# A decoder layer with 64 routed experts: three fp32r passes for gate, up and half of down, longer weight runs, skipped padding rows

## The chip, the cores and the metric

The kernel runs on one core of one Trainium2 chip, in one launch. The metric is the device time of that launch in microseconds; lower is better. All weights and activations are float32.

## The reference, cut to what matters

One decoder layer for 512 tokens of width 1024. A token mixer (an RG-LRU branch and an S5 branch from one input projection, joined by gates, one output projection, layer norm) is followed by a mixture of experts, a gated per-layer embedding, and a second layer norm. The change touches the S5 branch's small matmuls and the experts:

```python
combine = jnp.einsum('tk,tke->te', gate, one_hot(expert_idx, 64))   # 8 of 64 experts for each token
y = jnp.einsum('tf,fd->td', silu(xt @ ws_gate) * (xt @ ws_up), ws_down)          # shared expert
for c in range(64 // 8):
    g = jnp.einsum('td,edf->tef', xt, w_gate[sl])      # 1024 -> 256
    u = jnp.einsum('td,edf->tef', xt, w_up[sl])
    hdn = jax.nn.silu(g) * u * combine[:, sl, None]
    y = y + jnp.einsum('tef,efd->td', hdn, w_down[sl]) # 256 -> 1024
```

512 tokens with 8 experts each are 4096 pairs of a token and an expert. The kernel gives each expert one tile of 96 slots (SL), and further overflow tiles only where more than 96 tokens chose it; with these inputs no overflow tile runs.

## The kernel before, in words

Five engines and the DMA queues run their own instruction streams, written out by hand and joined by semaphores; what an engine does next is fixed by the order in its block. SyncE (SP) issues plain loads and stores, GpSimd (POOL) the indirect ones.

*First stage (0 to about 420 us).* The mixer's branches in NB = 4 blocks. In a block TensorE (from L769) does two of x_proj and g_proj(0), turns of U2 and R, the 64-row matmuls K (L802 to L811), g_proj(1), S (L815), g_proj(2), the gates' matmuls (L825, recorded at L833), then Y (L839 to L847: per group g one matmul over 128 rows, L843, and two over 64 rows, L844 and L845), then the next block's x_proj(b+1, 0), then the turn of Y (L855), which waits for Y_kept: four ScalarE copies (L1180) that stand in ScalarE's order behind the gates' sigmoids, the decays (Exp, Tanh, L1171) and the square roots (L1176), which themselves wait for VectorE (L1557) and GpSimd (L570, L572). x_proj and g_proj are already done in three fp32r passes (mm3, L676): a value is split into a high part, its fp32r rounding, and a low part, the rest; high x high, high x low and low x high are added up in PSUM. ScalarE makes the high parts, GpSimd (L536) and VectorE (L1291, called from low) the low ones. A plain fp32 matmul is issued as two instructions, so the 8 products of a 1024-long contraction are x16 in the trace; an fp32r pass is one.

*Second stage (to about 625 us).* The gated products of the mixer, b_product, in three fp32r passes. *Third stage (to about 818 us).* Output projection, layer norm, per-layer embedding, routing, shared expert (sh_in L921, sh_out L962). Routing writes the slot table: GpSimd stores (token, gate) pairs with 32 indirect DMAs (L605), reads the table back (L609), TensorE turns it (L989), and VectorE keeps it (tables_kept, L1748). Unused slots hold the indices T and up, which point at 96 padding rows of x1_dram and acc_dram; those rows are zeroed through yzero (L587, L600).

*Routed experts (from 819 us).* For expert u TensorE's order is gate_up(u) (L1005: 8 products of the rows, as 128x96 weights, with 512 columns of gate and up), x_turn(u+1) (L995), down(u-1) (L1023: two halves of 512 columns, two products each), hid_turn(u) (L1015). ScalarE: silu, half of the row copy (rows_kept), half of the y copy (y_kept). VectorE: the product with up and with the combine weight (L1785), the other halves, and the copy of the turned hidden rows (L1792). Gate, up and down have four buffers each: SP loads expert e+4's gate and up (L465) once g_e_put says that gate_up(e) is done, and its down (L468) after y_e_put. In DRAM a row of gate is 256 values; the buffer interleaves gate and up, so a run is 1 KB; down's runs are 4 KB. GpSimd gathers the 96 rows of expert e+4 (gather, L613) and adds the 96 rows of y to acc_dram (add_rows, L622), one add at a time: each waits for the one before to land. After the last add the sum is reloaded, normed and stored.

The store of acc to acc_dram (L487) is issued when the shared expert is done. The change puts a buffer over acc, and waits for it.

## Time and profile before

| | us |
|---|---|
| three runs | 1622.08, 1614.36, 1612.36 |
| median | 1614.36 |
| the profiled execution | 1616.47 |
| its span, first to last instruction | 1614.6 |
| TensorE busy | 1519.5 (94%) |
| TensorE weight loads busy (beside matmuls) | 855.5 (53%) |
| VectorE busy | 551.5 (34%) |
| ScalarE busy | 339.8 (21%) |
| GpSimd busy | 443.1 (27%) |
| HBM read and written | 297.35 MB, 35.44 MB |

Matmuls are pipelined and their ends are modelled, so the duration of one is longer than the distance to the next; where a rate matters, distances between starts are read. The busy shares are means over stages with different limits, so each part is read from its own stage. PEclk 1.00 is the 2.4 GHz level of TensorE's clock and 0.50 the 1.2 GHz level. DMA share is the mean over the 16 DMA engines of the time that packets took; packets of two queues overlap, so it can pass 1. In the views "issue" is time in which an engine waited for nothing that the profile shows.

### The profile page before, as it was taken

The page shows a single profiled execution, that of the slowest core. Times are in us where ns is not written, and L with a number is a line of the kernel's source. Part 1 is how long each engine was busy: PE and PEld are TensorE (multiplying, and loading weights), DVE is VectorE, ACT ScalarE, POOL GpSimd, SP SyncE. Part 2 cuts the span into 40 slices and gives each one's busy share as a digit, 9 for nine tenths or more (in the row PEclk, how much of TensorE's full clock was granted, in tenths as well). Part 3 has the DMA queues.
Part 4 walks back from the last instruction along what each step waited for, and adds up shares of the span by engine and source line. Part 5 has one row for each costly group of instructions (what it writes and reads, how often), then busy time and mean ns, then how long its engine had stood idle before and what let it go on. Part 6 is the DMA issues. An engine that isn't in the chain of part 4 may idle for free.

```text
span 1614.6 us, 16181 instructions
## 1 busy us (share of the span) xinstructions
PE 1519.5 (94%) x5781; PEld 855.5 (53%) x5781; DVE 551.5 (34%) x920; ACT 339.8 (21%) x527; POOL 443.1 (27%) x416
## 2 busy tenths in 40 slices
PE   7979999999999999999989999999999999999990
PEld 4456767676788886454434444444444444444440
DVE  4597877776410011448211111111111111111114
ACT  4115453537322221010001111111111111111110
POOL 2013433334534432001612222222222222222212
PEclk8999999999999999999999999999999999999996
DMA  8034243442333326700499999999999999999974
GB/s 231 0 118 66 66 66 82 77 77 67 90 93 105 98 85 249 281 14 0 160 331 327 335 326 323 327 341 327 322 318 317 325 327 326 330 330 319 335 228 124
DMA packets 258194, 333.49 MB, mean 207 GB/s; under 512 B 14834, under 2 KB 229570, under 8 KB 249504
## 3 DMA queue, kind: packets, MB, share of 16 engines
q1 hardware_dynamic: 242464, 281.50, 56.1%
q0 software_dynamic: 15680, 51.32, 13.1%
q8 instruction: 32, 0.52, 0.1%
q14 instruction: 18, 0.15, 0.0%
HBM read 297.35 MB, written 35.44 MB: 206 GB/s over the span
## 4 chain that ended last, share of the span: by engine, by line
PE 69%; DMA 13%; issue 6%; DVE 4%; POOL 3%; SPq 3%; ACT 1%; POOLq 1%; DVEq 1%; ACTq 0%
PE bank L1011 20%; DMA arena<-moe_w_up_in 12%; PE bank L1030 10%; PE bank L677 6%; PE bank L678 6%; PE bank L679 6%; PE bank L684 4%; PE bank L905 3%; PE bank L891 3%; PE bank L711 3%; POOL wa_low L536 2%; SPq L468 2%; PE bank L925 2%; DVE arena L1291 1%; DVE lru_low L1291 1%
## 5 line engine op out<-in xcount | busy, mean ns | idle before, releaser
L1011 PE MATMUL bank<-arena 128*96 128x512 f32 x1024 | 455.2, 598 | 20.4 <-DMA arena<-moe_w_up_in 19.4
L1088 ACT ACTIVATE arena<-bank 128x512 f32<-128x512 f32 (+6 forms) x312 | 163.3, 543 | 859.5 <-PE bank L1011 442.0
L1011 PEld LDWEIGHTS bank<-arena 128*96 128x96 f32 x1024 | 164.0, 165 | 265.4 <-issue 265.3
L1030 PE MATMUL bank<-arena 128*96 128x512 f32 x512 | 230.4, 592 | 1.0 <-DVE arena L1792 1.0
L1291 DVE TENSOR_TENSOR arena<-arena 128x512 f32<-128x512 f32 (+10 forms) x286 | 206.7, 754 | 31.3 <-POOLq L561 12.7
L1297 DVE SCALAR_TENSOR_TENSOR arena<-arena,bank 96x256 f32<-96x256 f32 (+1 forms) x72 | 36.0, 500 | 482.3 <-ACT arena L1088 451.4
L684 PEld LDWEIGHTS bank<-arena 96*128 96x128 f32 (+4 forms) x1001 | 127.9, 186 | 83.9 <-issue 82.5
L536 POOL TENSOR_TENSOR wb_low<-arena,wb_high 128x1024 fp32r<-128x1024 f32 (+1 forms) x40 | 106.5, 2665 | 149.9 <-ACT wb_high L1088 149.9
L626 POOL COPY arena<-arena 96x1 int32 (+1 forms) x64 | 11.5, 180 | 468.3 <-DVE arena L1780 423.3
L684 PE MATMUL bank<-arena 96*128 96x96 f32 (+4 forms) x1001 | 128.4, 267 | 10.6 <-DMA arena<-x_in 4.7
L1030 PEld LDWEIGHTS bank<-arena 128*96 128x96 f32 x512 | 80.3, 167 | 103.9 <-issue 103.9
L536 POOL TENSOR_TENSOR wa_low<-arena,wa_high 128x1024 fp32r<-128x1024 f32 x24 | 61.8, 2591 | 197.4 <-ACT wa_high L1088 197.4
L629 POOL DMA_INDIRECT acc_dram<-arena x64 | 94.3, 1473 | 55.1 <-POOL arena L626 50.5
L1780 DVE COPY arena<-bank 96x512 f32<-96x512 f32 x64 | 44.0, 687 | 185.3 <-PE bank L1030 167.8
L677 PE MATMUL bank<-x_high,wa_high 128*128 128x512 f32 x192 | 77.4, 403 | 8.1 <-DVE x_low L1291 7.9
L1297 DVE SCALAR_TENSOR_TENSOR arena<-bank,arena 128x511 f32<-128x511 f32 (+3 forms) x44 | 32.2, 747 | 139.5 <-PE bank L679 137.3
L1088 ACT ACTIVATE wb_high<-arena 128x1024 fp32r<-128x1024 f32 (+1 forms) x40 | 45.8, 1145 | 147.1 <-DMA arena<-w_glu_in 81.6
L678 PE MATMUL bank<-x_low,wa_high 128*128 128x512 f32 x192 | 75.4, 392 | 0.0
L679 PE MATMUL bank<-x_high,wa_low 128*128 128x512 f32 x192 | 75.3, 392 | 0.0
L618 POOL DMA_INDIRECT arena<-x_dram,arena x64 | 60.5, 945 | 51.6 <-POOL arena L615 51.6
L1088 ACT ACTIVATE arena<-arena 128x512 f32<-128x512 f32 (+5 forms) x54 | 32.0, 610 | 181.7 <-DVE arena L1597 88.0
L605 POOL DMA_INDIRECT slot_dram<-arena x32 | 31.8, 992 | 130.6 <-DVEq L1288 121.1
(146 smaller groups left out, 1758.0 us busy)
## 6 DMA issues: line engine op xcount, KB each, us to landing
arena<-moe_w_gate_in SPq DMA_DIRECT2D x64, 1024.0 KB, 14.2
arena<-moe_w_up_in SPq DMA_DIRECT2D x64, 1024.0 KB, 19.0
...
arena<-w_in_in SPq DMA_DIRECT2D x2, 2048.0 KB, 11.9
```

What stands on the lines that cost most here:

```text
L536: nc.gpsimd.tensor_tensor(lo, w, hi.bitcast(f32), ALU.subtract).then_inc(S["w_split"], 1)
L618: nc.gpsimd.indirect_dma_start(out=xg[u], out_offset=None, in_=x1_dram, in_offset=bass.IndirectOffsetOnAxis(ap=idxcol[:, u:u + 1].bitcast( ...
L629: nc.gpsimd.indirect_dma_start(out=acc_dram, out_offset=bass.IndirectOffsetOnAxis(ap=idxcol[:, 4:5].bitcast(u32), axis=0), in_=yb[buf], in ...
L677: mm(dst, w_hi, v_hi, start=start, stop=False)
L678: mm(dst, w_hi, v_lo, start=False, stop=False)
L679: return mm(dst, w_lo, v_hi, start=False, stop=stop)
L684: return nc.tensor.transpose(dst, src, ident[0:n, 0:n])
L1011: last = mm(banks[2 + u % 2][0:SL, :], xgT[u % 2][:, k, :], gu[u % 4][:, k, :, :], start=(k == 0), stop=(k == KD - 1))
L1030: last = mm(banks[5 + hf][0:SL, :], hT[u % 2][:, k, 0:SL], dn[u % 4][:, k, hf * 512:(hf + 1) * 512], start=(k == 0), stop=(k == 1))
L1088: return nc.scalar.activation(out_, in_, func, **kw)
L1291: return V_.tensor_tensor(out_, a, b_, op)
L1297: return V_.scalar_tensor_tensor(out_, a, s, b_, op0, op1)
```

## The change

- Gate, up and the first half (k = 0) of down's contraction go in three fp32r passes. Per expert ScalarE makes the high parts: four copies of 128x1024 for gate and up (gate_up_high), one for down (down_high), two of 128x384 for the rows (rows_high), one of 128x96 for the hidden rows; VectorE makes the low parts by subtraction in the same shapes, for the weights in place (gate_up_low, down_low, rows_low). The second half of down stays fp32. The high parts of gate and up have two buffers, the second over acc, so ScalarE waits for acc_stored ahead of its first expert; the turned rows have one buffer. gate_up_high(u+1) and gate_up_low(u+1) stand at the head of expert(u) on their engines.
- Gate, up and down are loaded in runs of 8 KB; the buffers of gate and up are no longer interleaved. This holds for the shared expert too.
- Padding rows are skipped: gather and add have a bounds check at T-1; the padding rows and their zeroing are gone, and GpSimd zeroes the four gather buffers once (96x4096), between slot_ready and the 32 stores of the slot table.
- On GpSimd the add of expert u-1 stands behind the gather of u+4, in place of the add of u.
- K's and Y's matmuls are reordered: Y does its 16 matmuls over 128 rows first, then the 64-row ones with the two halves of rows in turn; K likewise takes the halves in turn.

Its core (the rename of semaphores, the overflow branch and declarations are left out; `plain` is `part` with type float32):

```diff
-        gu = [at(o, KD * 2 * F).rearrange("p (k w f) -> p k w f", k=KD, w=2)
-              for o in (b1, tail, late + 4096, b0)]
-        dn = [at(o, 2 * D).rearrange("p (k c) -> p k c", k=2)
-              for o in (b1 + 4096, b0 + 6144, b1 + 6144, b0 + 4096)]
+        gu_at = (b1, tail, late + 4096, b0)
+        gu_raw = [plain(f"gate_up{n}", o, 2 * KD, F) for n, o in enumerate(gu_at)]
+        gu = [v.rearrange("p (w k) f -> p k w f", w=2) for v in gu_raw]
+        gu_row = [[v[:, w * KD:(w + 1) * KD, :].rearrange("p k f -> p (k f)") for w in range(2)] for v in gu_raw]
+        dn_at = (b1 + 4096, b0 + 6144, b1 + 6144, b0 + 4096)
+        dn = [plain(f"down{n}", o, 2, D) for n, o in enumerate(dn_at)]
+        dn_row = [v.rearrange("p k c -> p (k c)") for v in dn]
         xg = [at(late + n * D, D, SL) for n in range(4)]
-        xgT = [at(b1 + 8192 + n * KD * SL, KD * SL).rearrange("p (k s) -> p k s", k=KD) for n in range(2)]
+        xg_all = at(late, 4 * D, SL)
+        xgT = at(tail + 4096, KD * SL).rearrange("p (k s) -> p k s", k=KD)
+        xe_hi = part("rows_high", tail + 4096, KD, SL)
+        xe_lo = part("rows_low", tail + 4096 + KD * SL, KD, SL)
+        gu_hi = [part(f"gate_up_high{n}", o, 2 * KD, F) for n, o in enumerate((x_off, m_off))]
+        gu_lo = [part(f"gate_up_low{n}", o, 2 * KD, F) for n, o in enumerate(gu_at)]
+        dn_hi = [part(f"down_high{n}", o, 2, D) for n, o in enumerate((b1 + 8192, sg_off))]
+        dn_lo = [part(f"down_low{n}", o, 2, D) for n, o in enumerate(dn_at)]
+        he_hi = [part(f"hidden_high{n}", b1 + 10240 + 512 * n, 1, SL)[:, 0] for n in range(2)]
+        he_lo = [part(f"hidden_low{n}", b1 + 10240 + 512 * n + 128, 1, SL)[:, 0] for n in range(2)]
...
             def load_in(e, u, done):
                 for w, src in enumerate((w_gate_e, w_up_e)):
-                    sp.dma_start(gu[u][:, :, w, :], src[bass.ds(e, 1)].rearrange("o p k f -> p (o k) f")).then_inc(done, 16)
+                    sp.dma_start(gu_row[u][w], src[bass.ds(e, 1)].rearrange("o p x -> p (o x)")).then_inc(done, 16)
 
             def load_down(e, u, done):
-                sp.dma_start(dn[u], w_down_e[bass.ds(e, 1)].rearrange("o p k c -> p (o k) c")).then_inc(done, 16)
+                sp.dma_start(dn_row[u], w_down_e[bass.ds(e, 1)].rearrange("o p x -> p (o x)")).then_inc(done, 16)
...
+            pool.wait_ge(S["padded"], 16)
+            pool.wait_ge(S["res_put"], 2 * TT)
             pool.wait_ge(S["slot_ready"], 1)
+            nc.gpsimd.memset(xg_all, 0.0)
+            pool.drain()
             for t in range(TT):
                 for k in range(K):
                     nc.gpsimd.indirect_dma_start(
...
                 nc.gpsimd.indirect_dma_start(
                     out=xg[u], out_offset=None, in_=x1_dram,
-                    in_offset=bass.IndirectOffsetOnAxis(ap=idxcol[:, u:u + 1].bitcast(u32), axis=0)).then_inc(s_gath[u], 16)
+                    in_offset=bass.IndirectOffsetOnAxis(ap=idxcol[:, u:u + 1].bitcast(u32), axis=0),
+                    bounds_check=T - 1, oob_is_err=False).then_inc(s_gath[u], 16)
...
                 pool.sem_inc(S["col_seen"], 1)
                 nc.gpsimd.indirect_dma_start(
                     out=acc_dram, out_offset=bass.IndirectOffsetOnAxis(ap=idxcol[:, 4:5].bitcast(u32), axis=0),
-                    in_=yb[buf], in_offset=None, compute_op=ALU.add).then_inc(S["rows_added"], 16)
+                    in_=yb[buf], in_offset=None, bounds_check=T - 1, oob_is_err=False,
+                    compute_op=ALU.add).then_inc(S["rows_added"], 16)
...
             for u in range(4):
                 pool.wait_ge(S["xT_e_put"], u + 1)
                 gather(4 + u, u, 4 + u)
-                add_expert(0, u)
+                if u:
+                    add_expert(0, u - 1)
             with pool.Fori(1, E // 4 - 1) as i:
                 for u in range(4):
                     pool.wait_ge(S["xT_e_put"], 4 * i + (u + 1))
                     gather(4 * i + (4 + u), u, 4 * i + (4 + u))
-                    add_expert(i, u)
+                    add_expert(i, u - 1)
             for u in range(E - 4, E):
-                add_expert(0, u)
+                add_expert(0, u - 1)
+            add_expert(0, E - 1)
...
-                for g in range(GB):
-                    q, h = divmod(g, 2)
-                    hs = slice(h * NS, (h + 1) * NS)
-                    if g == 0:
-                        pe.wait_ge(S["RT_kept"], 4 * (b + 1))
+                pe.wait_ge(S["RT_kept"], 4 * (b + 1))
+                for q in range(QB):
                     for c in range(2):
-                        last = mm(banks[4 + 2 * h + q // 4][0:GP, (q % 4) * P:(q % 4 + 1) * P], bT[hs, c, b * QB + q, :],
-                                  Q[hs, c, q, 0:L, :], start=(c == 0), stop=(c == 1))
-                    if g % 8 == 7:
+                        for h in range(2):
+                            hs = slice(h * NS, (h + 1) * NS)
+                            last = mm(banks[4 + 2 * h + q // 4][0:GP, (q % 4) * P:(q % 4 + 1) * P],
+                                      bT[hs, c, b * QB + q, :], Q[hs, c, q, 0:L, :], start=(c == 0), stop=(c == 1))
+                    if q % 4 == 3:
                         last.then_inc(S["K_put"], 1)
...
-                for g in range(GB):
-                    q, h = divmod(g, 2)
-                    hs = slice(h * NS, (h + 1) * NS)
-                    dst = banks[4 + 2 * h + q // 4][0:NC, (q % 4) * P:(q % 4 + 1) * P]
-                    mm(dst, U[:, g, :], M[:, g, :], start=True, stop=False)
-                    mm(dst, hp[hs, 0, q, 0:NC], Q[hs, 0, q, 1:L + 1, :], start=False, stop=False)
-                    last = mm(dst, hp[hs, 1, q, 0:NC], Q[hs, 1, q, 1:L + 1, :], start=False, stop=True)
-                    if g % 8 == 7:
-                        last.then_inc(S["Y_put"], 1)
+                for q in range(QB):
+                    for h in range(2):
+                        mm(y_bank(h, q), U[:, 2 * q + h, :], M[:, 2 * q + h, :], start=(q % 4 == 0), stop=False)
+                for j in range(2):
+                    for c in range(2):
+                        for q in range(4 * j, 4 * j + 4):
+                            for h in range(2):
+                                hs = slice(h * NS, (h + 1) * NS)
+                                last = mm(y_bank(h, q), hp[hs, c, q, 0:NC], Q[hs, c, q, 1:L + 1, :],
+                                          start=False, stop=(c == 1 and q % 4 == 3))
+                    last.then_inc(S["Y_put"], 1)
...
             def gate_up(i, u):
 
-                pe.wait_ge(s_wgu[u % 4], 32 * i + 32 * (u // 4 + 1))
-                pe.wait_ge(S["xT_e_act"], 4 * i + u + 1)
-                pe.wait_ge(S["xT_e_dve"], 4 * i + u + 1)
+                pe.wait_ge(S["gu_e_low"], 16 * i + 4 * u + 4)
+                pe.wait_ge(S["xT_e_low"], 8 * i + 2 * u + 2)
+                whi = gu_hi[u % 2].rearrange("p (w k) f -> p k w f", w=2)
+                wlo = gu_lo[u % 4].rearrange("p (w k) f -> p k w f", w=2)
                 for k in range(KD):
-                    last = mm(banks[2 + u % 2][0:SL, :], xgT[u % 2][:, k, :], gu[u % 4][:, k, :, :],
-                              start=(k == 0), stop=(k == KD - 1))
+                    last = mm3(banks[2 + u % 2][0:SL, :], xe_hi[:, k], xe_lo[:, k], whi[:, k], wlo[:, k], k == 0, k == KD - 1)
                 last.then_inc(S["g_e_put"], 1)
 
...
 
             def down(i, u):
-                pe.wait_ge(s_wdn[u % 4], 16 * i + 16 * (u // 4 + 1))
-                pe.wait_ge(S["hT_e_kept"], 4 * i + u + 1)
+                pe.wait_ge(S["dn_e_low"], 4 * i + u + 1)
+                pe.wait_ge(S["hT_e_high"], 8 * i + 2 * u + 2)
+                pe.wait_ge(S["hT_e_low"], 4 * i + u + 1)
                 wait(pe, S["y_e_act"], 4 * i + u)
                 wait(pe, S["y_e_dve"], 4 * i + u)
                 for hf in range(2):
-                    for k in range(2):
-                        last = mm(banks[5 + hf][0:SL, :], hT[u % 2][:, k, 0:SL], dn[u % 4][:, k, hf * 512:(hf + 1) * 512],
-                                  start=(k == 0), stop=(k == 1))
+                    hs = slice(hf * 512, (hf + 1) * 512)
+                    mm3(banks[5 + hf][0:SL, :], he_hi[u % 2], he_lo[u % 2], dn_hi[u % 2][:, 0, hs], dn_lo[u % 4][:, 0, hs],
+                        True, False)
+                    last = mm(banks[5 + hf][0:SL, :], he[u % 2], dn[u % 4][:, 1, hs], start=False, stop=True)
                 last.then_inc(S["y_e_put"], 1)
 
...
-            def rows_kept(i, u):
+            def rows_high(i, u):
                 act.wait_ge(S["xT_e_put"], 4 * i + u + 1)
-                f(xgT[u % 2][:, 0:4, :], banks[0][:, 0:4 * SL].rearrange("p (k x) -> p k x", k=4), ACT.Copy).then_inc(S["xT_e_act"], 1)
+                for h in range(2):
+                    f(xe_hi[:, 4 * h:4 * h + 4], banks[h][:, 0:4 * SL].rearrange("p (k x) -> p k x", k=4),
+                      ACT.Copy).then_inc(S["xT_e_high"], 1)
+
+            def gate_up_high(i, u):
+                act.wait_ge(s_wgu[u % 4], 32 * i + 32 * (u // 4 + 1))
+                wait(act, S["g_e_put"], 4 * i + u - 1)
+                for k in range(2):
+                    for w in range(2):
+                        ks = slice(KD * w + 4 * k, KD * w + 4 * k + 4)
+                        f(gu_hi[u % 2][:, ks], gu_raw[u % 4][:, ks], ACT.Copy).then_inc(S["gu_e_high"], 1)
+
+            def down_high(i, u):
+                act.wait_ge(s_wdn[u % 4], 16 * i + 16 * (u // 4 + 1))
+                wait(act, S["y_e_put"], 4 * i + u - 1)
+                f(dn_hi[u % 2][:, 0], dn[u % 4][:, 0], ACT.Copy).then_inc(S["dn_e_high"], 1)
 
...
 
             def expert(i, u, more=True):
+                if more:
+                    gate_up_high(i, u + 1)
                 act.wait_ge(S["g_e_put"], 4 * i + u + 1)
-                wait(act, S["hid_e"], 4 * i + u - 1)
-                f(sil[u % 2][0:SL, :], banks[2 + u % 2][0:SL, 0:F], ACT.Silu).then_inc(S["silu_e"], 1)
+                wait(act, S["hT_e_put"], 4 * i + u - 1)
+                f(hid_e[u % 2], banks[2 + u % 2][0:SL, 0:F], ACT.Silu).then_inc(S["silu_e"], 1)
                 if more:
-                    rows_kept(i, u + 1)
+                    rows_high(i, u + 1)
+                down_high(i, u)
                 if not isinstance(i, int) or u >= 1:
                     y_kept(i, u - 1)
-
-            rows_kept(0, 0)
+                act.wait_ge(S["hT_e_put"], 4 * i + u + 1)
+                wait(act, S["y_e_put"], 4 * i + u - 1)
+                f(he_hi[u % 2], banks[4][:, 0:SL], ACT.Copy).then_inc(S["hT_e_high"], 1)
+                f(he[u % 2], banks[4][:, SL:2 * SL], ACT.Copy).then_inc(S["hT_e_high"], 1)
+
+            act.wait_ge(S["slot_ready"], 1)
+            gate_up_high(0, 0)
+            rows_high(0, 0)
+            act.wait_ge(S["acc_stored"], 16)
             for u in range(0, 5):
                 expert(0, u)
...
-            def rows_kept(i, u):
-                dve.wait_ge(S["xT_e_put"], 4 * i + u + 1)
-                V_.tensor_copy(xgT[u % 2][:, 4:8, :], banks[1][:, 0:4 * SL].rearrange("p (k x) -> p k x", k=4)).then_inc(S["xT_e_dve"], 1)
+            def rows_low(i, u):
+                for h in range(2):
+                    ks = slice(4 * h, 4 * h + 4)
+                    dve.wait_ge(S["xT_e_high"], 8 * i + 2 * u + h + 1)
+                    tt(xe_lo[:, ks], banks[h][:, 0:4 * SL].rearrange("p (k x) -> p k x", k=4), xe_hi[:, ks].bitcast(f32),
+                       ALU.subtract).then_inc(S["xT_e_low"], 1)
+
+            def down_low(i, u):
+                dve.wait_ge(S["dn_e_high"], 4 * i + u + 1)
+                tt(dn_lo[u % 4][:, 0], dn[u % 4][:, 0], dn_hi[u % 2][:, 0].bitcast(f32), ALU.subtract).then_inc(S["dn_e_low"], 1)
+
+            def gate_up_low(i, u):
+                for k in range(2):
+                    for w in range(2):
+                        ks = slice(KD * w + 4 * k, KD * w + 4 * k + 4)
+                        dve.wait_ge(S["gu_e_high"], 16 * i + 4 * u + 2 * k + w + 1)
+                        tt(gu_lo[u % 4][:, ks], gu_raw[u % 4][:, ks], gu_hi[u % 2][:, ks].bitcast(f32),
+                           ALU.subtract).then_inc(S["gu_e_low"], 1)
...
             def expert(i, u, more=True):
+                if more:
+                    gate_up_low(i, u + 1)
                 dve.wait_ge(S["silu_e"], 4 * i + u + 1)
-
-                stt(hdn[u % 2][0:SL, :], sil[u % 2][0:SL, :], gateT[:, bass.ds(4 * i + u, 1)],
+                stt(hid_e[u % 2], hid_e[u % 2], gateT[:, bass.ds(4 * i + u, 1)],
                     banks[2 + u % 2][0:SL, F:2 * F], ALU.mult, ALU.mult).then_inc(S["hid_e"], 1)
                 if more:
-                    rows_kept(i, u + 1)
+                    rows_low(i, u + 1)
+                down_low(i, u)
                 if not isinstance(i, int) or u >= 1:
                     y_kept(i, u - 1)
-                dve.wait_ge(S["hT_e_put"], 4 * i + u + 1)
-                V_.tensor_copy(hT[u % 2][:, :, 0:SL], banks[4][:, 0:2 * SL].rearrange("p (k x) -> p k x", k=2)).then_inc(S["hT_e_kept"], 1)
-
-            rows_kept(0, 0)
+                dve.wait_ge(S["hT_e_high"], 8 * i + 2 * u + 2)
+                tt(he_lo[u % 2], banks[4][:, 0:SL], he_hi[u % 2].bitcast(f32), ALU.subtract).then_inc(S["hT_e_low"], 1)
+
+            gate_up_low(0, 0)
+            rows_low(0, 0)
             for u in range(0, 5):
                 expert(0, u)
```

## Rows read from the trace of the kernel before

**Rows 1.** The page, 40 slices of the span: GB/s moved by DMA in each.

```profile
GB/s 231 0 118 66 66 66 82 77 77 67 90 93 105 98 85 249 281 14 0 160 331 327 335 326 323 327 341 327 322 318 317 325 327 326 330 330 319 335 228 124
```

**Rows 2.** Chain of waits, start of the routed experts: start us, us, what.

```profile
806.79 3.71 PE bank L978 x8
...
821.51 9.27 PE bank L1011 x16
...
832.37 7.08 PE bank L1011 x16
...
840.30 3.44 PE bank L1030 x8
...
843.94 6.87 PE bank L1011 x16
```

**Rows 3.** Chain of waits, end of the execution: expert 63's last gate/up matmul ends.

```profile
1570.41 3.45 PE bank L1030 x8
```

**Rows 4.** Stages: us, busy (x) PE PEld DVE ACT POOL, PEclk, DMA share, GB/s.

```profile
614.00:622.00 8.00, 8.00 (x37) 6.61 (x36) 0.46 (x1) 1.97 (x2) 1.52 (x1) 1.00 1.02 415
780.00:790.00 10.00, 8.96 (x23) 4.10 (x22) 2.04 (x4) 0.38 (x1) 7.76 (x8) 1.00 1.08 369
820.00:825.00 5.00, 4.26 (x9) 1.71 (x8) 0.56 (x1) 0.49 (x1) 0.10 (x1) 0.50 1.09 317
850.00:1150.00 300.00, 300.00 (x902) 133.01 (x901) 50.42 (x106) 38.87 (x80) 72.82 (x104) 1.00 1.07 330
1150.00:1550.00 400.00, 380.50 (x1120) 167.82 (x1119) 62.64 (x132) 48.23 (x99) 91.26 (x130) 1.00 1.07 325
```

**Rows 5.** Waits, 850 to 1560 us: us in total, times, longest.

```profile
PE bank L1011 <- DMA arena<-moe_w_up_in: 19.4, 23, 1.9
```

**Rows 6.** TensorE in order of time, product with w_lru_out: 24 matmuls between.

```profile
560.08 0.39 PE L677 MATMUL bank<-s_high,wb_high 128*128 128x512 f32 x1
...
565.52 0.39 PE L677 MATMUL bank<-lru_high,wb_high 128*128 128x512 f32 x1
```

**Rows 7.** DMA queues, 1150 to 1550 us: packets, MB, share of 16 engines.

```profile
q1 hardware_dynamic: 73481, 103.93, 79.9%
q0 software_dynamic: 7391, 25.94, 26.6%
```

**Rows 8.** Groups by form, whole execution: busy us, mean ns, idle before.

```profile
L1088 ACT ACTIVATE wb_high<-arena 128x1024 fp32r<-128x1024 f32 x32 | 33.9, 1059 | 115.9 <-DMA arena<-w_glu_in 81.6 <-DMA arena<-w_in_in 34.3
...
L1291 DVE TENSOR_TENSOR arena<-arena 128x1024 f32<-128x1024 f32 x43 | 51.6, 1223 | 3.1 <-issue 0.9
...
L1775 DVE COPY arena<-bank 128x384 f32<-128x384 f32 x64 | 35.1, 548 | 3.0 <-PE bank L684 3.0
...
L1291 DVE TENSOR_TENSOR lru_low<-arena,lru_high 128x512 fp32r<-128x512 f32 x12 | 17.2, 1503 | 0.0
```

**Rows 9.** The page, DMA issues: queue, count, KB each, us from issue to landing.

```profile
acc_dram<-arena SPq DMA_DIRECT2D x1, 2048.0 KB, 16.4
...
acc_dram<-arena POOLq DMA_INDIRECT x64, 8.8
```

**Rows 10.** GpSimd, then VectorE, in order of time: zeroing, token table, shared expert's end.

```profile
630.48 0.95 POOL L587 MEMSET arena<- 96x1024 f32 x1
...
804.15 0.62 POOL L609 DMA_DIRECT2D arena<-slot_dram  x1 [1.42 <-DMA slot_dram<-arena]
...
816.50 1.28 DVE L1291 TENSOR_TENSOR arena<-arena,bank 128x512 f32<-128x512 f32 x2 [3.79 <-PE bank L978]
```

**Rows 11.** Block 1 in order of time: K, Y's first, next product, Y's copies.

```profile
193.42 3.68 PE L808 MATMUL bank<-arena 64*16 64x128 f32 x64 [0.94 <-ACT arena L1088]
...
222.40 0.43 PE L843 MATMUL bank<-arena 128*64 128x128 f32 x2
...
237.44 0.50 PE L677 MATMUL bank<-x_high,wa_high 128*128 128x512 f32 x1
...
240.68 2.04 ACT L1088 ACTIVATE arena<-bank 64x512 f32<-64x512 f32 x4
```

65 lines of the change are left out of this document (34 added, 31 removed).

## The prediction

> **What bounds the kernel now.** I read the 40 slices of the page first: the last 31 of them, from about 760 us on, hold a stretch in which the DMA engines move 320 to 340 GB/s without a break [rows 1]. That is the routed experts. The chain of waits through their start gives the beat: gate and up of one expert are 16 fp32 instructions in 6.87 us, the turn of the next rows 0.86 (from 839.45, the end of one gate/up, to 840.30), down 3.44, the turn of the hidden rows 0.20 (from 843.74 to 843.94), so 11.37 us of TensorE per expert, back to back [rows 2]. From expert 1's first gate/up matmul (832.37) to expert 63's last (1570.41 [rows 3]) there are 62 periods and one gate/up: (738.0 - 6.9) / 62 = 11.79 us. The stages say who sets it: TensorE is busy for all of 850 to 1150, but for only 380.5 of the 400 us after it, while the DMA share stays at 1.07 [rows 4]; the missing 19.4 us are waits for moe_w_up [rows 5]. One expert moves 3 x 1.049 MB of weights and 2 x 0.393 MB of gathered and scattered rows, 3.93 MB; at 325 GB/s that is 12.1 us. So DMA at 12.1 is the limit, TensorE at 11.37 lies just under it, and the buffers hide the difference for the first 26 experts (26 x 0.7 = 18 us). Both must fall for the time to fall.
>
> **TensorE per expert, after.** An fp32 instruction takes 6.87 / 16 = 0.429 us, two per product. An fp32r product of the same 512 columns comes every (565.52 - 560.08) / 24 = 0.227 us [rows 6]. Gate/up becomes 24 x 0.227 = 5.45. Down becomes 6 x 0.227 for the first half of its contraction and 4 x 0.429 for the second, 3.08. The turns stay, 1.06. Sum 9.59 us, against 11.37. With 96 weight columns in place of 128 the 0.227 may be a little less; 0.2135, half of an fp32 instruction, gives 9.18, the lower end.
>
> **DMA per expert, after.** Queue 1 moves 260 GB/s (103.9 MB in 400 us) in a share of 0.799, queue 0 65 GB/s in 0.266: 325 and 244 GB/s per unit of share, 1.065 in all [rows 7]. With expert loads almost alone (1 KB runs for two thirds of the bytes) the trace shows 369 at 1.08, or 342 per unit; with the 4 KB runs of w_out alone 415 at 1.02, or 407 [rows 4]. I carry over the same loss beside queue 0 (325/342 = 0.95): 8 KB runs then go at 387 per unit, 3.146 / 387 = 8.13 us. 512 tokens in 8 experts each are 4096 rows, 64 per expert of 96, and no overflow tile ran, so skipping leaves 0.524 MB: 2.15 us. (8.13 + 2.15) / 1.065 = 9.65 us. Bounds: nothing lost beside queue 0, 9.3; runs of no effect and only the skipping, (9.68 + 2.15) / 1.065 = 11.1; neither effect, 12.1. I take 9.65, since rows at both run lengths exist.
>
> **ScalarE and VectorE per expert.** In 850 to 1150 they are busy 38.9 and 50.4 us over 26.4 experts, 1.47 and 1.91 each [rows 4]. ScalarE gains four highs of gate/up and one of down at 1.06, one more row copy at 0.55 (VectorE's for the same shape), and two 96-column copies (estimate 0.3 each, under the 0.55 for 384 columns): 1.47 + 5.3 + 0.55 + 0.6 = 7.9 us. VectorE gains five lows at 1.22 and one more half of the rows at 0.55; the hidden copy only changes: 1.91 + 6.1 + 0.55 = 8.6 us [rows 8]. Both are under 9.6. What matters too is the loop through them, since each runs in order: down(u-1) ends, y copy 0.6, hidden copies 0.6, first high 1.06, four lows 4.9, gate product 0.48, two row lows 1.1, some 0.4 of semaphores: 9.1 us to the start of gate/up(u+2). TensorE takes 0.2 + 5.45 + 0.86 + 3.08 + 0.2 = 9.8 for the same stretch. 0.7 us are left, so the lows are hidden, but a low of 1.4 us in place of 1.22 would no longer be. The serial scatter is as close: 8.8 us to landing plus some 1.0 us of column copy and semaphore [rows 9] is 9.8 at 96 rows; for 64 rows the 8.8 lies between two thirds of it, 5.9, and all of it, and I take 7.5, so 8.5. Deferring it by one expert on GpSimd costs nothing: two y buffers cover it.
>
> With three limits between 9.1 and 9.7 they disturb each other; buffers hide some 18 us of DMA lag as before. I take a period of 9.8 us.
>
> **The start of the routed stage.** gate_up_low(0,0) stands on VectorE behind the shared expert (done at 817.8 [rows 10]): four lows to 822.7, row lows to 823.8, so gate/up(0) starts at 823.9 and not 821.5. Then ScalarE waits for acc_stored before it may write the high parts of expert 1 over acc. That store is issued at 821.0 and takes 16.4 us to land [rows 9], 837.4; ahead of it were the loads of experts 2 and 3, which now go faster, so I take 833.5. Then four highs (4.2), silu 0.4, product after the last low 1.7, row lows 1.1: gate/up(1) starts at 840.6, 8.2 later than 832.37. TensorE idles some 8 us and restarts at the lower clock: after the gap at 819 the granted clock was 0.50 in 820 to 825 [rows 4], the 1.2 GHz level, and gate/up(0) took 9.27 in place of 6.87 [rows 2]. I add 2. The memset of 96x4096 before the 32 token stores is 4 x 0.95 = 3.8 us [rows 10]; the token table's read, issued by 804.8 and landed some 2 us later (my estimate), then lands at about 810.6, and TensorE asks for it at 810.5 [rows 2, 10], so 0 (if that cover is gone, up to 4 us). The dropped zero stores were off the path.
>
> **K and Y by row halves.** K: 64 instructions in 3.68 us, 0.0575 each; a 128-column fp32 instruction at the rate of the long ones would be 0.107, so the halves overlap already, and reordering gives 0 (at most 3.68 - 64 x 0.0535 = 0.3 per block). Y: 16 groups from 222.40 to 237.44, 0.94 us each. New: 32 full instructions at 0.107 and 64 half ones at K's rate, 3.4 + 3.7 = 7.1 us in place of 15.0. But what follows is x_proj(b+1,0), 5.45 us, and then the turn of Y, which waits for ScalarE's four copies, 240.68 to 242.72: their start comes from the chain of decays and square roots, not from Y [rows 11]. TensorE arrived at 242.9 before, and will arrive at 235.0 and wait 7.7 us. So of 4 x 7.9 = 32 us, 0.2 per block remain, and the idle time costs a restart at the lower clock, 1 to 3 us each (the shape of 820 to 825). Net for this stage: +3 us (bounds -4 and +10). The shared expert only changes its layout.
>
> **Sum.** Expert 63's gate/up ends at 842.6 + 62 x 9.8 + 5.45 = 1455.7; first stage +3; tail as before 1614.6 - 1570.4 = 44.2. Span 1502.9. The profiled execution took 1616.47, 1.87 outside its span, and lies 2.1 above the median of 1614.36: 1502.9 + 1.9 - 2.1 = 1502.7, say **1502 us**. In general: 895 + 62T.
>
> **The rivals.**
> - *DMA stays the bound* (0.17): 8 KB runs bring less beside gathers. T of 10.3 to 10.9 after the buffers' share: 1534 to 1571. For it: 1.07 all along; the 415 was without queue 0. Against: the sum above. A cap on all traffic together, whatever its runs, is the same rival seen otherwise: at 350 GB/s, midway between the 330 of the routed stage and the 369 of loads alone [rows 4], 3.67 MB take 10.5 us, less 0.3 hidden 10.2, and the time is 1527; 0.05 of the 0.17, since w_out's load reached 415. The Trainium skill states such a cap (DMA: Bandwidth & Descriptors, Specifications): HBM gives a core about 358 GB/s; by it 3.67 MB would take 10.25 us. If skipped rows cost as before (the change not doing what it says), (8.13 + 3.22) / 1.065 = 10.7, less 0.3 hidden: 1540.
> - *The loop of ScalarE and VectorE, or the scatter* (0.17): lows at 1.4 to 1.6 us, or 9.8 of scatter kept whole with GpSimd held up. T 10.1 to 10.8: 1521 to 1565. For it: VectorE 90% full, in strict order.
> - *Faster than forecast* (0.08): 9.18 of TensorE and DMA near 9.3, T 9.35: 1475.
> - *Slower than before* (0.05): lows lengthened by GpSimd beside them. The lru_low lows, 0.68 us alone, took 1.50 on average beside GpSimd's subtractions [rows 8]. At T = 11.6 the gain is gone; that is lows of (11.6 - 2.5) / 5 = 1.8 us. At twice the price, 2.4, T = 14.5 and the time is 1794. Against it: beside experts GpSimd runs only one-column copies and descriptor writing.
> - *The forecast*, T 9.5 to 10.1: 0.53.
>
> **How the numbers follow.** Range 1476 to 1562: it leaves out the slower rival and the ends of the others. Faster by over 1% (about what a measurement of this kernel can tell from no change) takes all but the slow rival and T between 11.3 and 11.9: 0.92; within 1% 0.04; slower 0.04.
>
> **What would show it.** Right: gate/up in 5.3 to 5.5 us, down near 3.1, rate near 375 GB/s, period 9.6 to 10, gate/up(1) starting some 8 us later, Y near 7 us followed by a TensorE wait for ScalarE of 7 to 8 us. Wrong: TensorE waiting for VectorE's gate_up_low at each expert (loop), ScalarE waiting for moe_w_up (DMA), lows above 1.4 us, or a first stage shorter by over 5 us.

## The result, and the profile after

The kernel after the change takes 1589.7 us (median of four runs, 1586.16 to 1593.05) where the kernel before takes 1614.3: a ratio of 0.983, 95% interval 0.980 to 0.986. The direction was forecast, the size was not: 1502 us was given, with 1562 as the upper end. The profiled execution has a span of 1591.2 us, 88.3 above the 1502.9 of the sum.

The page of the kernel after, slices and queues [rows 1]:

```profile
PEclk7999898989999999999997999999999999999995
DMA  8034242425133334810246999999999999999953
GB/s 235 0 106 80 67 68 67 67 54 106 53 106 99 86 106 165 330 76 1 84 170 211 344 348 344 336 333 337 323 337 328 332 340 322 334 326 330 325 147 118
DMA packets 141492, 315.98 MB, mean 199 GB/s; under 512 B 18898, under 2 KB 100514, under 8 KB 116160
...
gate_up<-moe_w_gate_in SPq DMA_DIRECT2D x64, 1024.0 KB, 12.4
gate_up<-moe_w_up_in SPq DMA_DIRECT2D x64, 1024.0 KB, 26.2
```

Packets fell from 258194 to 141492 and the bytes from 333.5 to 316.0 MB, so both DMA parts do what they say; yet the routed stage still moves 330 GB/s and not 375. (The prediction speaks of the last 31 slices of the page before; from 760 us on it is some 21 of them.)

Stages after, columns as in [rows 4]:

```profile
850.00:1150.00 300.00, 274.58 (x1188) 179.96 (x1188) 218.01 (x273) 187.62 (x304) 92.09 (x104) 0.98 0.92 322
1150.00:1450.00 300.00, 276.74 (x1189) 178.70 (x1188) 212.72 (x272) 182.31 (x298) 93.56 (x108) 1.00 0.94 331
```

TensorE now idles 8%, and the DMA share is 0.94 where it was 1.07. Nothing in this row looks full. The waits of the same 300 us (us in total, times, longest):

```profile
POOL arena L647 <- DMA acc_dram<-arena: 156.4, 27, 6.3
DVE gate_up_low L1346 <- ACT gate_up_high L1118: 86.8, 27, 3.7
ACT gate_up_high L1118 <- DMA gate_up<-moe_w_up_in: 79.6, 27, 3.4
ACT arena L1118 <- DMA acc_dram<-arena: 38.1, 27, 2.4
```

Two things are late at every expert: the add of the expert before (POOL and ScalarE's y copy wait for it) and the up weights (ScalarE's high parts wait for them, and VectorE and TensorE behind it). The chain of waits names only the first; it ended

```profile
1498.29 8.95 DMA acc_dram<-arena
1507.47 1.10 POOL arena L647
1508.71 0.51 issue
1509.45 9.28 DMA acc_dram<-arena
1518.96 0.36 POOL arena L647
```

and says 37% of the whole span is adds landing. From one add to the next: about 9.1 us of landing and 1.8 of copy, semaphores and issue, 10.9, which is the period. From this I took theory A, that the serial chain of adds sets the period. It was wrong, as two_acc shows below.

The start of the routed experts, TensorE and ScalarE in order of time (start us, us, ..., idle before):

```profile
827.23 1.03 PE L707 MATMUL bank<-arena 106*96 106x106 f32 x4 [5.75 <-DMA arena<-slot_dram]
...
841.00 0.71 PE L700 MATMUL bank<-gate_up_high,rows_high 128*96 128x512 f32 x1 [4.42 <-DVE rows_low L1346]
...
854.26 3.90 ACT L1118 ACTIVATE gate_up_high<-gate_up 128x1024 fp32r<-128x1024 f32 x4 [16.77 <-DMA acc_dram<-arena]
...
861.46 0.71 PE L700 MATMUL bank<-gate_up_high,rows_high 128*96 128x512 f32 x1 [0.43 <-DVE rows_low L1346]
```

The token table is 5.75 us late, and ScalarE waits 16.77 us for the accumulator's store before it may write the high parts of expert 1.

The 88.3 us come apart by the prediction's own steps. Gate/up of expert 1 starts at 861.46, the sum had 845.6: 15.9. Gate/up of expert 63 starts at 1539.21, so the period is (1539.21 - 861.46) / 62 = 10.93 and not 9.8: 70.1. Its own length and the tail, 1591.2 - 1544.8 = 46.4 for 44.2: 2.3.

### The profile page after: what moved, and what is told of

It reads as the page before. It is cut to its first block, busy times and chain, and to the rows that moved or that the text cites. A ratio compares the mean times of both kernels' runs of the same rounds, so it can differ in the third digit from the quotient of the medians.

```text
span 1591.2 us, 19168 instructions
## 1 busy us (share of the span) xinstructions
PE 1422.4 (89%) x6421; PEld 958.7 (60%) x6421; DVE 921.3 (58%) x1304; ACT 678.3 (43%) x1039; POOL 493.1 (31%) x414
## 2 busy tenths in 40 slices
DMA packets 141492, 315.98 MB, mean 199 GB/s; under 512 B 18898, under 2 KB 100514, under 8 KB 116160
## 4 chain that ended last, share of the span: by engine, by line
DMA 38%; PE 36%; issue 8%; POOL 6%; DVE 5%; ACT 2%; POOLq 2%; DVEq 1%; SPq 0%; ACTq 0%
DMA acc_dram<-arena 37%; PE bank L700 8%; PE bank L701 7%; PE bank L702 7%; PE bank L918 3%; POOL arena L647 3%; PE bank L734 3%; POOL slot_dram L625 2%; DVE arena L1346 2%; PE bank L707 2%; PE bank L932 2%; ACT arena L1118 1%; POOLq L591 1%; PE bank L833 1%; POOL arena L592 1%
## 5 line engine op out<-in xcount | busy, mean ns | idle before, releaser
L1346 DVE TENSOR_TENSOR gate_up_low<-gate_up,gate_up_high 128x1024 fp32r<-128x1024 f32 x256 | 296.5, 1221 | 193.4 <-ACT gate_up_high L1118 193.4
L1118 ACT ACTIVATE gate_up_high<-gate_up 128x1024 fp32r<-128x1024 f32 x256 | 249.7, 1048 | 178.7 <-DMA gate_up<-moe_w_up_in 161.9
L700 PE MATMUL bank<-gate_up_high,rows_high 128*96 128x512 f32 x512 | 208.4, 407 | 29.1 <-DVE rows_low L1346 29.1
L702 PE MATMUL bank<-gate_up_high,rows_low 128*96 128x512 f32 x512 | 203.9, 398 | 0.0
L701 PE MATMUL bank<-gate_up_low,rows_high 128*96 128x512 f32 x512 | 202.5, 396 | 0.0
L647 POOL COPY arena<-arena 96x1 int32 (+1 forms) x64 | 46.9, 733 | 375.9 <-DMA acc_dram<-arena 360.3
L1061 PE MATMUL bank<-down,arena 128*96 128x512 f32 x256 | 130.6, 592 | 0.0
L700 PEld LDWEIGHTS bank<-gate_up_high,rows_high 128*96 128x96 f32 x512 | 83.6, 163 | 69.6 <-DVE rows_low L1346 31.5
L702 PEld LDWEIGHTS bank<-gate_up_high,rows_low 128*96 128x96 f32 x512 | 83.4, 163 | 36.8
L701 PEld LDWEIGHTS bank<-gate_up_low,rows_high 128*96 128x96 f32 x512 | 83.8, 164 | 32.5
```

What stands on the lines that cost most here:

```text
L647: nc.gpsimd.tensor_copy(idxcol[:, 4:5].bitcast(i32), idxT[:, bass.ds(e, 1)].bitcast(i32)).then_inc(S["sc_col"], 1)
L700: mm(dst, w_hi, v_hi, start=start, stop=False)
L701: mm(dst, w_hi, v_lo, start=False, stop=False)
L702: return mm(dst, w_lo, v_hi, start=False, stop=stop)
L1061: last = mm(banks[5 + hf][0:SL, :], he[u % 2], dn[u % 4][:, 1, hs], start=False, stop=True)
L1118: return nc.scalar.activation(out_, in_, func, **kw)
```

## The experiments

Fifteen runs in four groups; a ratio is to the kernel before on the same chip, with its 95% interval. The chips differ by up to 1.2% (1614.3 to 1633.0 us for the kernel before), so kernels of different groups are compared by ratio. The period P is the time between adds, from 950 to 1450 us (first to last issue over their number less one); by that measure the kernel before has 11.87 and the kernel after 11.09 (10.93 over the whole stage, since the first experts live on loaded buffers).

| kernel | us | ratio (interval) | P |
|---|---|---|---|
| the kernel after | 1589.7 | 0.983 (0.980 to 0.986) | 11.09 |
| no_add | 1525.7 | 0.934 (0.930 to 0.939) | 9.74 |
| two_acc | 1608.9 | 0.986 (0.981 to 0.991) | 11.08 |
| y_old | 1597.1 | 0.978 (0.973 to 0.982) | 11.19 |
| short_runs | 1600.6 | 0.981 (0.976 to 0.986) | 11.14 |
| half_down | 1530.2 | 0.935 (0.930 to 0.940) | 9.73 |
| pad_rows | 1603.9 | 0.981 (0.978 to 0.985) | 11.25 |
| interleaved | 1631.1 | 1.000 (0.998 to 1.003) | 11.60 |
| before_dma | 1604.9 | 0.982 (0.979 to 0.986) | 11.37 |
| spread | 1534.2 | 0.951 (0.947 to 0.955) | 10.21 |
| start_fix | 1570.5 | 0.974 (0.970 to 0.978) | 11.08 |
| best3 | 1512.2 | 0.937 (0.933 to 0.940) | 10.18 |
| best3_again | 1526.7 | 0.937 (0.934 to 0.940) | 10.14 |
| best4 | 1536.1 | 0.942 (0.939 to 0.946) | 10.18 |
| pad_spread | 1605.6 | 0.984 (0.980 to 0.988) | 11.19 |
| before_spread | 1603.3 | 0.983 (0.979 to 0.986) | 11.36 |

(no_add issues no adds; its P is from the first high part of expert 1, at 863.2, to that of expert 63, at 1467.4.)

**First group: is it the chain of adds?** The kernel before took 1633.0 us on this chip.

no_add:

```diff
-                nc.gpsimd.indirect_dma_start(out=acc_dram, ..., compute_op=ALU.add).then_inc(S["rows_added"], 16)
+                pool.sem_inc(S["rows_added"], 16)
```

> The kernel after the change without the transfer that adds an expert's rows into the accumulator in DRAM (its semaphore is raised by GpSimd itself; the output then lacks the routed experts' part). Theory A: the period of 10.93 us an expert is the serial chain of these adds (landing 9.1 us, then 1.8 us until the next is issued). Without them the period falls to what TensorE needs, 9.6 to 9.9 us, and the whole to 1510 to 1530 us. Rival B: the experts' weights arrive too late, or ScalarE's and VectorE's loop is longer than worked out: the period stays at 10.6 us or more and the whole at 1565 us or more.

1525.7 us, P 9.74; TensorE is busy for all 300 us of the stage. A's numbers, but the run took two things away together, the chain and the adds' traffic. What the traffic is, the queues' shares from 1150 to 1450 us show, after first, then no_add:

```profile
q1 hardware_dynamic: 11710, 85.28, 75.4%
q0 software_dynamic: 6063, 13.94, 18.9%
```

```profile
q1 hardware_dynamic: 13290, 96.82, 85.8%
q0 software_dynamic: 3472, 8.03, 8.3%
```

16 x 300 x 0.189 us over 1.70 thousand rows moved each way (13.94 MB in rows of 4 KB, half of them adds) and 16 x 300 x 0.083 over 1.96 thousand gathered alone give 0.20 us of an engine for a gathered row and some 0.33 for an added one, against 0.35 for 8 KB of weights. An added row costs as much as twice its bytes of weights.

two_acc:

```diff
-    out=acc_dram, out_offset=...idxcol[:, 4:5]...).then_inc(S["rows_added"], 16)
+    out=(acc_dram, acc2_dram)[par], out_offset=...idxcol[:, 4 + par:5 + par]...).then_inc(s_add[par], 16)
```

> The kernel after the change with the same adds, going by turns into two accumulators in DRAM, each with its own semaphore and column of indices, so that an add waits for the one before the last. The second accumulator is zeroed by 2 MB of stores ahead of the experts, read back at the end and added on VectorE. All the traffic of the adds stays. Theory A (the serial chain): period 9.7 to 10.2 us, the whole 1530 to 1560 us, some 3 us of it for the zeroing and the last sum. Rival B (the adds' traffic, the weights or the engines' loop bound the period): 10.7 us or more, the whole 1585 us or more.

1608.9 us, P 11.08: B's numbers. The chain is gone, and ScalarE waits for the weights in its place, 105.5 us where it was 79.6:

```profile
POOL arena L653 <- DVE arena L1856: 157.8, 27, 7.4
ACT gate_up_high L1125 <- DMA gate_up<-moe_w_up_in: 105.5, 27, 4.9
```

So the chain that the view showed was a follower: the serial adds fill the period they are given. Why one add takes 9 us to land is another question, and no run answers it: in before_dma below it takes 9.6 us at a DMA share of only 0.89.

short_runs:

```diff
-  sp.dma_start(gu_row[u][w], src[bass.ds(e, 1)].rearrange("o p x -> p (o x)"))
+  sp.dma_start(gu_raw[u][:, w * KD:(w + 1) * KD, :], src[bass.ds(e, 1)].rearrange("o p k f -> p (o k) f"))
```

> The kernel after the change with the experts' weights loaded in runs of 1 KB (gate, up) and 4 KB (down), as before, into the new layout. Theory A1: the short runs cost the DMA engines what they cost before, so the weights need 11.3 to 11.8 us an expert and the whole is 1610 to 1645 us, and the add's landing is not what sets the period. Theory A2: the long runs gave nothing, since the serial chain sets the period anyway, and they lengthen the adds' landings (one of their 4 KB rows waits behind 8 KB packets): with short runs an add lands in 8 us or less, the period is 9.9 to 10.5 us and the whole 1530 to 1565 us. Rival: the length of the runs matters to neither, 1587 to 1595 us.

A miss of the experiment: the page has 141492 packets, those of the kernel after. Both sides are contiguous, and the runs are merged however the view is written. It serves as a second run of the kernel after, on this chip 1600.6 us. The question went to interleaved.

y_old:

```diff
-  for q in range(QB):
-      for h in range(2):
-          mm(y_bank(h, q), U[:, 2 * q + h, :], M[:, 2 * q + h, :], start=(q % 4 == 0), stop=False)
...
+  for g in range(GB):
+      q, h = divmod(g, 2)
+      mm(dst, U[:, g, :], M[:, g, :], start=True, stop=False)
+      mm(dst, hp[hs, 0, q, 0:NC], Q[hs, 0, q, 1:L + 1, :], start=False, stop=False)
+      last = mm(dst, hp[hs, 1, q, 0:NC], Q[hs, 1, q, 1:L + 1, :], start=False, stop=True)
```

> The kernel after the change with the old order of the products into the K and Y banks in the first stage. If the new order costs the first stage 2.7 us in each of its four blocks, as the starts of K in the two traces say (75.3 us from block to block against 72.6), the whole falls by 8 to 11 us, to 1579 to 1583 us, and block to block is 72.6 us again. Rival: the stage's extra comes from elsewhere (the granted clock in its first slices): the whole stays at 1587 to 1592 us.

Block to block it is 72.6 us again (K at 123.41, 196.06, 268.68, 341.30; in short_runs 121.37, 196.69, 272.02, 347.34). The stage 100 to 400 us, after, then y_old:

```profile
100.00:400.00 300.00, 264.56 (x1787) 202.62 (x1786) 210.57 (x258) 136.34 (x188) 108.73 (x59) 0.94 0.38 73
```

```profile
100.00:400.00 300.00, 292.66 (x1818) 210.13 (x1817) 225.21 (x267) 143.72 (x198) 110.89 (x60) 1.00 0.38 73
```

The quicker Y leaves TensorE idle, and the granted clock falls to a mean of 0.94: in block 1 of the kernel after the products are 0.23 us apart before the wait that ends at 247.91 and 0.43 after it (250.40 to 250.83), the 1.2 GHz level. From K to K that loses 2.7 us, and 8.1 over the three steps between the four blocks; after the last block nothing more is lost (423.2 us from K to the slot table's clearing, 422.9 from K to its first store in the kernel before). The whole fell by 3.4 us against short_runs, inside both intervals: ScalarE's high parts of expert 1 began some 6 us earlier (860.4 for 866.7), since y_old's first block began 2 us later, and the rest was not seen at the end. The block times show the mechanism; the 8 to 11 us that were expected of the total are not shown.

**Second group: which part of the DMA load?** Before: 1630.8 us. Theory D takes the place of A: the packets of the DMA engines bound the stage.

half_down:

```diff
-  load_down(4 * i + (4 + u), u, s_wdn[u])
+  sp.dma_start(dn_row[u][:, 0:D], w_down_e[bass.ds(4 * i + (4 + u), 1), :, 0:D]...).then_inc(s_wdn[u], 16)
```

> The kernel after the change, but from the fifth expert on only the first half of each down matrix is loaded (512 KB in place of 1 MB; the second half of the output's contraction then uses old weights). Everything else, the chain of adds too, stays. Theory D: the packets of the DMA engines bound the routed stage: 8.24 us (weights) and 2.07 us (rows) an expert, 10.3 of the period of 10.93. With 1.4 us of weights less, TensorE is the bound: period 9.7 to 9.9 us, the whole 65 to 75 us shorter than after the change. Theory A (the serial chain of adds, as long as measured): the period stays at 10.6 to 10.9 us.

1530.2 us, P 9.73, with all adds in their chain, and TensorE busy for 300.00 of 300 us. Theory A falls here a second time: with less weight traffic the chain shortens by itself. The DMA share was 0.94 here too, as in the kernel after, so that share does not tell whether the DMA is the bound:

```profile
1150.00:1450.00 300.00, 300.00 (x1358) 203.82 (x1357) 252.85 (x309) 210.63 (x341) 123.89 (x123) 1.00 0.94 323
```

pad_rows:

```diff
-  nc.gpsimd.memset(xg_all, 0.0)
+  for dst in (x1_dram, acc_dram): nc.gpsimd.dma_start(dst[T:T + SL, :], yzero)...
-  bounds_check=T - 1, oob_is_err=False
```

(the last line at the gather and at the add)

> The kernel after the change without its skipping: the rows of padding are gathered and added as before (96 rows an expert in place of 64). Theory D: 32 rows more in each direction, in packets of 0.327 us (adds) and 0.194 us (gathers) on 16 engines, are 1.04 us an expert: period 11.8 to 12.1 us, the whole 55 to 70 us longer than after the change. Theory A: only what the landing of an add grows by counts (8.8 us at 96 rows before the change): period 10.9 to 11.3 us.

D misses: 1603.9 us beside 1600.6 for the kernel after (short_runs), and a period of 11.25 for 11.14. A's range, 10.9 to 11.3 us, holds that period, but two_acc and half_down had already ruled A out. Moving half as many rows again costs about 0.1 us an expert and nothing clear of noise in the whole:

```profile
1150.00:1450.00 300.00, 273.61 (x1180) 177.11 (x1178) 208.02 (x266) 178.99 (x291) 96.50 (x108) 1.00 1.02 350
```

Here the same rate of weights stands beside a share of 1.02 and 350 GB/s, so the 0.94 and 331 of the kernel after were not a ceiling on either mean. Skipping took 6 to 8 points of share away, and nobody used them. That suggested engines that are free while others are full.

interleaved:

```diff
-  gu = [v.rearrange("p (w k) f -> p k w f", w=2) for v in gu_raw]
+  gu = [v.rearrange("p (k w) f -> p k w f", w=2) for v in gu_raw]
```

> The kernel after the change with gate and up interleaved in SBUF as before, so that their loads go in runs of 1 KB again (short_runs kept the packets as they were, 141492 of them, and was a second run of the kernel after the change). High and low parts are still taken from 1024 columns in a row. Theory D: the weights' packets take 9.4 us an expert again, as before the change, in place of 8.24: period 11.2 to 12.1 us, the whole 15 to 70 us longer. Theory A: the run length doesn't matter, period 10.8 to 11.0 us.

1631.1 us, P 11.60, level with the kernel before: without the long runs the change gains nothing. The period lies in the middle of D's range and the time, some 30 us over the kernel after by ratio, in its lower half.

before_dma: the 8 KB runs and the skipping, as in the change's own diff, in the kernel before, with the four row buffers cleared ahead of the wait for the slots.

> The kernel before the change with the two DMA parts of the change alone: runs of 8 KB and skipped padding rows (with the clearing of the four row buffers, put ahead of the wait for the slots). The experts' products stay plain fp32, the first stage stays as it was. Theory D: the DMA engines then need 10.3 to 10.9 us an expert, TensorE 11.37 is the bound, the period 11.4 us in place of 11.79: 24 us less than before, a ratio of 0.983 to 0.987, which is all that the whole change brought. Rival: the gain of the change comes from the three passes, and these two parts bring under 10 us (ratio over 0.993).

Ratio 0.982, P 11.37, TensorE busy for 300.00 of 300 us, as forecast: two edits of the DMA bring as much as the whole change. That does not make the rest of the change worthless in the routed stage: its period is 0.28 us shorter (11.09 for 11.37), some 17 us over 62 experts. What it loses elsewhere, 8.1 us in the first stage and the late start that start_fix repairs, uses that up.

**Third group: are the engines loaded unevenly?** Before: 1615.9 us.

spread:

```diff
+  nc.gpsimd.tensor_copy(slotV.rearrange("p (a b) v -> p a b v", a=16),
+                        slotR.rearrange("p (b a) v -> p a b v", a=16))
-  last = tp(banks[1][0:SL, v * P:v * P + NT], slotR[:, :, v], NT)
+  last = tp(banks[1][0:SL, v * P:v * P + NT], slotV[:, :, v], NT)
```

> The kernel after the change with the rows of each expert laid over the 96 partitions in another order: slot s goes to row 6 (s mod 16) + s div 16 (one copy of the token table, 96 x 2 columns, on GpSimd), so that the 64 rows in use stand in every group of six rows and not in the first 64. Theory E (skipped rows leave some of the 16 DMA engines free and the others as full as before): skipping has brought nothing so far (pad_rows: 11.07 us an expert at a DMA share of 1.02, the kernel after 10.95 at 0.94) because an indirect transfer gives each engine a block of neighbouring rows, and the weights, which need all 16, wait for the full ones. Spread out, every engine carries two thirds of the rows: period 9.8 to 10.3 us, add landing under 8.5 us, the whole 40 to 70 us shorter than after the change. Rival F (rows are dealt to the engines one by one, and the weights' queue is slowed by something else, such as bytes of DRAM): period 10.8 to 11.1 us, the whole within 8 us of after the change.

1534.2 us, ratio 0.951, P 10.21. The adds from 950 to 1450 us, in the kernel after and in spread (count, duration, first and last start):

```profile
L650 POOL DMA_INDIRECT acc_dram<-arena x45: 1469/1469/1471, 954.0 to 1442.0; - x45
```

```profile
L655 POOL DMA_INDIRECT acc_dram<-arena x49: 1464/1464/2193, 955.6 to 1445.7; - x49
```

The same rows, in another order of partitions, are worth 0.9 us an expert. Rival F falls. One forecast of E missed: an add lands in 8.7 us, not under 8.5, so the landing fell by only 0.4 us from 9.1, though by E the fullest engine carries a third fewer rows. Its stage and queues:

```profile
1150.00:1450.00 300.00, 293.85 (x1303) 197.30 (x1302) 235.29 (x294) 199.86 (x326) 99.70 (x119) 1.00 1.02 364
```

```profile
q1 hardware_dynamic: 12901, 93.95, 81.3%
q0 software_dynamic: 6502, 15.10, 20.6%
```

The share is 1.02 again as in pad_rows, now with 12% more weights (93.95 MB for 84.10) in the place of the padding.

start_fix:

```diff
-  pool.wait_ge(S["slot_ready"], 1)
   nc.gpsimd.memset(xg_all, 0.0)
   pool.drain()
+  pool.wait_ge(S["slot_ready"], 1)
...
-  load_expert(3, 3, ...); sp.wait_ge(S["sh_done"], TT); sp.dma_start(acc_dram ..., acc)
+  for t in range(TT): sp.wait_ge(S["sh_done"], t + 1); sp.dma_start(acc_dram[t * P:(t + 1) * P, :], acc[:, t, :])
+  sp.wait_ge(S["sh_y_put"], TT); load_expert(3, 3, ...)
```

> The kernel after the change with three moves at the start of the routed experts: the clearing of the row buffers ahead of the wait for the slots, the accumulator's store cut into its four tiles and issued as each is done, and the load of expert 3 behind it. If the start costs what the trace says (3.5 us of clearing, 16 us of ScalarE's wait for a store that stood behind 3 MB of weights), gate/up of expert 1 starts 12 to 18 us earlier, and the whole falls by 10 to 16 us. Rival: the weights bound the stage from the first expert on, and a later load of expert 3 only moves the wait: the whole within 5 us of after the change.

Ratio 0.974 against the change's 0.983, some 15 us. Gate/up of expert 1 starts at 842.21, 19 us earlier; 2.9 of them are this run's first block, which began earlier (K at 120.36 for 123.24), and 16 the edit's, as forecast. ScalarE's wait for the store is 1.9 us and not 16.8:

```profile
842.21 0.48 PE L701 MATMUL bank<-gate_up_high,rows_high 128*96 128x512 f32 x1 [1.12 <-DVE rows_low L1347]
```

best3: spread, start_fix and y_old together.

> The kernel after the change with spread, start_fix and the old order of K and Y together. Theory E: about 1520 to 1540 us where the kernel before takes 1614 (ratio 0.94 to 0.955): first stage 10 us less, start 12 less, period 9.8 to 10.2. Rival F: ratio 0.965 to 0.975.

1512.2 us, ratio 0.937: faster than both kernels, some 5% under the kernel after, and a little better than E's range of ratios (0.94 to 0.955).

**Fourth group: what is left, and whose is the gain?** Before: 1628.8 us.

best4: best3 with the edit of two_acc.

> best3 with the adds going by turns into two accumulators, as in two_acc. Theory G (with the rows spread out, the serial chain of adds, 8.7 us of landing and some 1.5 more, is what is left of the period of 10.2 us: in best3 ScalarE's copy of y waits 2.95 us an expert for the add before): period 9.8 to 9.9 us, the whole 10 to 20 us under best3, less some 3 us for the last sum. Rival H (the DMA engines, at a share of 1.02, are the bound at 10.2 us, and the wait for the adds only shows it): period 10.1 to 10.3 us, the whole 0 to 6 us over best3.

best3_again:

> best3 once more, for the comparison with best4 on one chip: a ratio of 0.933 to 0.940 to the kernel before.

best4 1536.1 and best3_again 1526.7 us: 9.4 slower, P 10.18 and 10.14. In best3 ScalarE's y copy had waited 2.95 us an expert for the add before; in best4 that wait is gone and the weights are late more often (69.3 us where best3 had 16.2):

```profile
ACT gate_up_high L1129 <- DMA gate_up<-moe_w_up_in: 69.3, 29, 3.4
```

H holds for the period (the price of the second accumulator is higher than I gave): at 10.2 us the DMA is the bound, and not the chain of adds.

pad_spread: pad_rows with the edit of spread.

> pad_rows (96 rows moved for each expert) with the order of the rows of spread. Theory E (skipping pays only where the engines share it): with nothing skipped the order of the rows can't matter, period 11.1 to 11.3 us, the whole within 8 us of pad_rows (ratio 0.98). Rival: the new order itself helps (other tokens beside each other in a transfer): period 10.2 to 10.7 us, ratio 0.95 to 0.965.

1605.6 us, P 11.19: with nothing skipped the order is worth nothing. It is the skipping that the order sets free.

```profile
1150.00:1450.00 300.00, 274.41 (x1182) 177.77 (x1182) 209.16 (x267) 179.80 (x294) 96.59 (x108) 1.00 1.02 351
```

before_spread: before_dma with the edit of spread.

> before_dma (the kernel before with 8 KB runs and skipped rows, products in plain fp32) with the order of the rows of spread. TensorE needs 11.37 us an expert there and was busy all the time already: the period stays 11.37 us and the ratio 0.980 to 0.985. So what the three passes bring shows only against this kernel: spread stands at 0.951. Rival: the DMA still held before_dma back: ratio under 0.975.

0.983, P 11.36, as before_dma. So with the rows spread the rest of the change, the three passes above all, is worth 0.983 to 0.951, over 3%; without it, nothing in the whole (0.982 for before_dma, 0.983 for the kernel after).

## Why the prediction was wrong, point by point

**The bound before.** Right: DMA and TensorE side by side. before_dma, with only the DMA relieved, runs at TensorE's 11.37, the figure worked out from [rows 2].

**TensorE after, 9.59 us.** Right. A product every 0.23 us (24 from 1106.94 to 1112.59 us, 5.65 for 5.45), down 3.2, and no_add and half_down, where nothing else binds, run at 9.74 and 9.73.

**DMA after, 9.65 us: the step that failed.** It is made of two terms, each the time at a share of 1. The weights: taken as 8.13 us; measured a share of 0.754 at a period of 11.09 us, 8.36. The rows: 2.15 us; measured 0.189 of 11.09, 2.10. Both are right within 3%. What failed is the division of their sum by 1.065, the share that the kernel before had reached, as if all 16 engines could be had for any mix. The kernel after reached 0.94, and (8.36 + 2.10) / 0.94 is 11.1. The runs show that this loss hangs on where the used rows lie: the period is nearly that of pad_rows (11.09 to 11.14, and 11.25), so the prediction's step "skipping leaves 0.524 MB: 2.15 us" bought next to nothing, and with the same rows spread out it is 10.21. Of the 70 us, spread gives back (11.09 - 10.21) x 62 = 55. The rest, 10.2 for 9.8, is (8.3 + 2.1) us at the share of 1.02 that was reached, not 1.065. The bound "only the skipping, 11.1" in the prediction meets the measured period by chance: it supposes that long runs have no effect, and interleaved shows that they are worth 0.5 us an expert.

The likely mechanism is that each engine serves a block of neighbouring partitions: with the used rows in the first partitions some engines carry as many rows as with padding and the others few, and a load of weights is complete when its last engine is. It is inferred from spread, pad_rows, pad_spread and before_spread. The views give the 16 engines as one mean, so no row shows one of them, and it stays open whether it is the engine or something else that goes by partition. The Trainium skill (DMA: Bandwidth & Descriptors, The descriptor swizzle) states that in a transfer of 128 partitions each engine writes a fixed set of them, in neighbouring fours; the runs fit such a map for transfers of 96, and none shows it.

**The rivals.** "DMA stays the bound", T of 10.3 to 10.9, was the one that came true, and its last case, "if skipped rows cost as before", 10.7 and 1540 us, came nearest; I gave it only a part of 0.17. Its reason in the text was wrong (a change that does not do what it says): the skipped rows were not moved (13.94 MB on queue 0 in 300 us for 20.77 in pad_rows), and the time did not fall with them. The cap on all traffic, 350 GB/s, did not show: spread moves 364 GB/s for 300 us. The Trainium skill (DMA: Bandwidth & Descriptors, Specifications) gives about 358 GB/s for the HBM of one core. Here the figure is no ceiling: spread and best3_again (363) hold more for 300 us, and [rows 4] has 415 for 8 us. Whether the memory has a part in the 10.2 us that are left, no run tells.

**ScalarE, VectorE, the scatter.** The lows took 1.22 us and the highs 1.05, as taken; the loop fits into 9.73 us (half_down). The scatter's landing was taken as 7.5 us for 64 rows and was 9.1. That looks like the fault and is not what sets the period: two_acc takes the wait for it away and keeps the period. The landing hardly depends on the rows at all, 9.2 us with 96 of them (pad_rows) and 8.7 with 64 spread out; what makes it so long stays open.

**The start, +8.2 and +2.** Forecast 845.6, measured 861.46. The store was to land at 833.5, some 12 us after its issue; it was issued at 835.41, behind expert 3's load of 834.09, and landed 18.8 us later. The memset, "so 0 (if that cover is gone, up to 4 us)" in the prediction, cost all of it: the stores into the slot table start 15.3 us later than before (776.85 for 761.52). Of these 4.5 are the memset and the pause behind it (772.40 to 776.85), 8.1 the slower first stage, and 2.4 were there at the first block already (K at 123.24 for 120.82), a difference that K's start shows between runs of equal code too. start_fix gives back 16 us of the start, 15 in the whole.

**K and Y.** K unchanged, right (3.67 us). Y 3.71 + 3.71 = 7.4 us for the 7.1 worked out, then a wait of 7.39 us for ScalarE, for 7.7: right to the row. The price of the idle time, "1 to 3 us each", was 2.7 at each of the three steps from block to block, 8.1 in all, where the sum had +3; that is inside its bounds of -4 and +10.

**The chances.** The forecast had 0.53 and a range of 1476 to 1562. The mistake behind both is one: the limits were each worked out as means over engines and time, and all came to 9.8 or less. The rest of the miss, 15.9 us of the 88.3, was the start.
